# A two-block transformer kernel on one core: the first half's attention placed ahead of the state space inputs, scan and far projections

## What is computed

```python
h = rms_norm(concat([meta, x]), pre_mix_g)          # 16 + 1024 tokens
q1, q2, k1, k2, v, u = split(h @ w_in)              # four 64-wide heads, two branches each; u is 512 wide
q1, q2, k1, k2 = rope(...)
o = softmax(q1 k1) v - lam * softmax(q2 k2) v       # causal, then rms_norm
# state space model, 32 groups of 16 channels, 64 complex states each
x_t = A x_{t-1} + B u_t                              # scan over all 1040 tokens
y_t = Re(C x_t) + D u_t                              # then gelu, gate, rms_norm
x = x + rms_norm(concat([o, y]) @ w_out)             # then a gated feed-forward
# block two: retention | RWKV-7 | feed-forward | per-layer gate
for t in tokens:                                     # RWKV-7, 8 heads of 64
    sa = S @ (-kk_t)
    S = S * w_t + outer(sa, b_t) + outer(v_t, k_t)
    y_t = S @ r_t
```

## Time and profile before

| | us |
|---|---|
| median of 3 runs | 3780.99 (3775.95 to 3783.14) |
| the profiled execution | 3778.1 |
| its span, first to last instruction | 3776.3 |
| PE busy, share of span | 3229.1, 86% |
| DVE | 1729.2, 46% |
| ACT | 940.8, 25% |
| POOL | 1967.0, 52% |

### The profile page before, as it was taken

How to read it: one execution, slowest core, us unless ns; L and a number is a source line. 1 busy time by engine, 2 the same in 40 slices (tenths; PEclk the granted TensorE clock), 3 DMA queues, 4 the chain that set the end, 5 groups by cost and what they waited for, 6 DMA issues and landing times.

```text
span 3776.3 us, 48065 instructions
## 1 busy us (share of the span) xinstructions
PE 3229.1 (86%) x19536; PEld 2501.1 (66%) x19536; DVE 1729.2 (46%) x2399; ACT 940.8 (25%) x1665; POOL 1967.0 (52%) x1076
## 2 busy tenths in 40 slices
PE   5975587769999786988999998898899998899997
PEld 3654355547677564766777776676677777677885
DVE  6214623344443263186655555266566456322233
ACT  3110111233233223113223322413223322210012
POOL 4234111325455463664656566474567665667773
PEclk9886687879999897998999999999899999999998
DMA  3422122312222232422222214332222221322221
GB/s 110 84 79 71 51 61 61 102 67 69 83 67 67 73 134 101 146 92 70 68 71 78 72 61 157 111 118 84 70 67 83 77 83 64 123 84 94 95 96 62
DMA packets 144364, 321.57 MB, mean 85 GB/s; under 512 B 25904, under 2 KB 62960, under 8 KB 144144
## 3 DMA queue, kind: packets, MB, share of 16 engines
q1 hardware_dynamic: 58752, 213.94, 17.5%
q10 hardware_dynamic: 85392, 104.57, 8.8%
HBM read 277.68 MB, written 40.76 MB: 84 GB/s over the span
## 4 chain that ended last, share of the span: by engine, by line
PE 73%; DVE 16%; ACT 4%; ACTq 2%; issue 2%; DMA 2%; POOL 1%; DVEq 0%; POOLq 0%
PE ps L1680 29%; PE ps L1709 12%; PE ps L1721 11%; PE ps L1911 3%; PE ps L1455 3%; PE ps L1544 2%; DVE acc_dense L2088 1%; DVE act_lo L2088 1%; DVE ffh_lo L2761 1%; PE ps L1572 1%; ACTq L883 1%; DVE xn_dense L2095 1%; DVE local L2088 1%; DVE rq L2088 1%; PE ps L1618 1%
## 5 line engine op out<-in xcount | busy, mean ns | idle before, releaser
L522 POOL TENSOR_TENSOR w_hi<-w_raw,ones 128x1024 fp32r<-128x1024 f32 x408 | 799.3, 1959 | 1406.4 <-DMA w_raw<-weights 1392.2
L524 POOL TENSOR_TENSOR w_lo<-w_raw,w_hi 128x1024 fp32r<-128x1024 f32 x408 | 1005.7, 2465 | 32.0
L1680 PE MATMUL ps<-act_hi,w_hi 128*128 128x512 f32 x1696 | 711.1, 419 | 7.2 <-DVE act_lo L2088 6.6
L1680 PE MATMUL ps<-act_lo,w_hi 128*128 128x512 f32 x1696 | 685.2, 404 | 0.0
L1680 PE MATMUL ps<-act_hi,w_lo 128*128 128x512 f32 x1696 | 680.7, 401 | 0.0
L1680 PEld LDWEIGHTS ps<-act_hi,w_hi 128*128 128x128 f32 x1696 | 328.5, 194 | 100.9 <-issue 15.7
L1680 PEld LDWEIGHTS ps<-act_hi,w_lo 128*128 128x128 f32 x1696 | 327.7, 193 | 76.7
L1680 PEld LDWEIGHTS ps<-act_lo,w_hi 128*128 128x128 f32 x1696 | 327.9, 193 | 67.9 <-issue 1.7
L2088 DVE TENSOR_TENSOR acc_dense<-acc_dense,ps 128x512 f32<-128x512 f32 x352 | 241.9, 687 | 242.3 <-PE ps L1709 182.3
L1709 PE MATMUL ps<-w_hi,ffh_hi 128*128 128x512 f32 x704 | 298.0, 423 | 57.0 <-DVE acc_dense L2088 54.9
L626 ACT ACT_TABLE_LOAD x204 | 261.7, 1283 | 295.0 <-PE ps L1680 104.8
(11 more groups left out here) (381 smaller groups left out, 4765.2 us busy)
## 6 DMA issues: line engine op xcount, KB each, us to landing
w_raw<-weights SPq DMA_DIRECT2D x408, 512.0 KB, 3.5
rw<-rw_t ACTq DMA_DIRECT2D x24, 256.0 KB, 2.4
rw<-lora_t ACTq DMA_DIRECT2D x24, 256.0 KB, 2.0
row<-x ACTq DMA_DIRECT2D x8, 512.0 KB, 3.6
row_dense<-x ACTq DMA_DIRECT2D x8, 512.0 KB, 3.9
res<-row_dense ACTq DMA_DIRECT2D x8, 512.0 KB, 2.6
row_mix<-res ACTq DMA_DIRECT2D x8, 512.0 KB, 6.8
res<-row_mix ACTq DMA_DIRECT2D x8, 512.0 KB, 4.6
```

Of the source, the lines that this page charges most:

```text
L522: pool.tensor_tensor(w_hi[:, s], raw, ones[:, 0:1].to_broadcast([P, 1024]), MUL).then_inc(w_hi_made, 1)
L524: pool.tensor_tensor(w_lo[:, s], raw, w_hi[:, s].bitcast(F32), SUB).then_inc(w_ready, 1)
L1680: mm = pe.matmul(out, ws[w][:, s, P * k:P * k + P], acts[a][:, k, x], start=(k, w, a) == (0, 0, 0), stop=(k, w, a) == (KT - 1, 1, 0))
```

## The change

- `PROJ` keeps `v` and the near q and k pieces. All of `u` moves into `FAR`, in front of the far `v` and q, k: 12 pieces of `u`, 4 of `v`, 8 of q and k. The near pieces of attention come first in the weight order.
- `ssm()`: the tables `g_t` are turned in the same 8 steps as `kd`, copied to `gt_out` and stored to memory (`gt_scratch`). The input steps, the scan and the output steps all run between steps of `attention(0)`: inputs at steps 18 to 25, scan at 26 to 36, first tables at 37, outputs at 38, 42, ... 66.
- `HEAD_EVENTS`: 8 far pieces ahead of step 0, two per step up to step 13, then 49 over the next 50 steps.
- `u_scratch` is stored in two parts per unit (66 and 64 columns of each of 8 phases), since the far half of `u` comes later. The gather of `u_in` is issued by ACT behind the first far `v` piece.
- One semaphore, `tables_stored`, for all three tables; `kd` and its banks are single, not double.
- RWKV: `rw_off_product` and `rw_merge` go round the four quarters of the array instead of two; one ACT copy of 512 columns (`zi`) takes the place of an ACT and a DVE copy of 256. `rw_parts` is reordered: 32 of its 48 products go round four quarters, 16 round two.

```diff
-    PROJ = ([("u", m, s) for m in range(4) for s in range(3)] + [("v", i, 0) for i in (*range(HALF), NT)]
-            + [("qk", m, s) for m in range(8) for s in spans_of(m)])
+    PROJ = [("v", i, 0) for i in (*range(HALF), NT)] + [("qk", m, s) for m in range(8) for s in spans_of(m)]
...
-    FAR = [("v", i) for i in range(HALF, NT)] + [("qk", m) for m in range(8)]
+    FAR = [("u", m, s) for m in range(4) for s in (0, 2)] + [("u", m, 1) for m in range(4)] + [("v", i, 1) for i in range(HALF, NT)] + [("qk", m, 1) for m in range(8)]
...
-    PROJ_EVENTS = ["proj", "ssm"] + ["proj"] * 3 + ["ssm", "proj"] * TB + ["proj"] * 3 + ["ssm", "ssm", "proj", "proj"] * TB
+    PROJ_EVENTS = ["proj", "ssm"] + ["proj"] * 5 + ["ssm", "proj"] * TB + ["proj"] * 5
...
-        events, done = ["heads"] + ["far"] * 3, 3
-        extra = [["ssm"]] * (SCAN_PARTS + 1) + ([[]] * 5 + [["ssm"]]) * TB
+        events, done = ["heads"] + ["far"] * 8, 8
+        extra = [[]] * 18 + [["ssm"]] * (TB + SCAN_PARTS + 2) + ([[]] * 3 + [["ssm"]]) * (TB - 1)
+        early = 14
         for n in range(ATT_STEPS - 1):
-            now = min(4 * len(FAR) + 1, 3 + (4 * len(FAR) - 2) * (n + 1) // (ATT_STEPS - 5))
+            now = 8 + 2 * (n + 1) if n < early else min(FAR_PIECES, 8 + 2 * early + (FAR_PIECES - 8 - 2 * early) * (n + 1 - early) // (ATT_STEPS - 5 - early))
...
                 elif kind == "v":
                     spills_landed(0)
                     act.wait_ge(*far_done(n))
-                    give(fn(v_o[:, :], ps[:, m % 2, :], ACT.Copy), proj_kept)
+                    give(fn(v_o[:, :], ps[:, n % 2, :], ACT.Copy), proj_kept)
                     spill(t["v_scratch"][m], v_o[:, :], 0)
+                    if n == FAR_U:
+                        spills_landed(0, 1)
+                        for e in range(OCT):
+                            act.dma_start(u_in[SG * e:SG * e + SG], t["u_scratch"][:, :, e, :].rearrange("m (g h) c -> h (m g) c", h=SG)).then_inc(ssm_landed, 16)
+                        load_input_factors(0)
...
-            chunk_products(1, (off16, n_t)[n], inv)
-            for u in range(4):
-                for c in range(2):
-                    mm = pe.matmul(ps[head(c), 7, CH * u:CH * u + CH], inv[head(c), u], ident[head(c), head(c)], start=True, stop=True)
+            for lhs, rhs, at in (((off16, n_t)[n], inv, 0), (inv, None, P)):
+                for j in range(2):
+                    for side in range(2):
+                        u = 2 * side + j
+                        for c in range(2):
+                            right = ident[head(c), head(c)] if rhs is None else rhs[head(c), u]
+                            mm = pe.matmul(ps[head(c ^ side), 5 + 2 * side, at + CH * j:at + CH * j + CH], lhs[head(c), u], right, start=True, stop=True)
...
-        def rw_off_product(v, n):
-            dve.wait_ge(rw_mm, nth("mm", f"z{n}", v))
-            mark(dve.tensor_copy(xt[0][:, :, :], units(bank(1, 0, 256))), rw_dve, nth("dve", f"z{n}", v))
```

More of the change, by code:

```diff
@@ L168, in proj_done, with ends_far @@
         if ends_unit(kind, m, s):
-            return unit_done, {"u": U_SSM + m, "v": U_V + 3, "qk": U_QK + m}[kind] + 1
+            return unit_done, AT[0, U_V + 3 if kind == "v" else U_QK + m] + 1
         return proj_psum, sum(not ends_unit(*p) for p in PROJ[:n + 1])
     PROJ_COUNT = sum(not ends_unit(*p) for p in PROJ)
+    def ends_far(kind, m, s):
+        return {"u": s == 1, "v": m == NT - 1, "qk": True}[kind]
     def far_done(n):
[L176 to L179, removed]
+        kind, m, _ = FAR[n]
+        if not ends_far(*FAR[n]):
+            return proj_psum, PROJ_COUNT + sum(not ends_far(*f) for f in FAR[:n + 1])
+        return unit_done, AT[{"u": (0, U_SSM + m), "v": (1, U_V + 3), "qk": (1, U_QK + m)}[kind]] + 1
     def rope_index(m, s):
@@ L690, in project @@
                 src = ps[:, n % 3, 0:c1 - c0]
[L691 to L705, removed]
+                if kind == "v":
+                    if n:
+                        spills_landed(0)
                     rows = META if m == NT else P
@@ L730, in project_far @@
             act.dma_start(rope[:, :, 0:BANK], t["rope"][:, :, NEAR:L]).then_inc(const_landed, 16)
[L731 removed]
+            for n, (kind, m, s) in enumerate(FAR):
                 if kind == "qk" and m >= 2:
                     store_far(m - 2)
[L734 to L736 removed]
+                if s != 2:
+                    for part in range(3):
+                        yield
+                if kind == "u":
+                    if s != 2:
+                        spills_landed(m % 2)
+                    act.wait_ge(*far_done(n))
+                    c0, c1 = SPANS[s]
+                    o0, o1 = {0: (META // OCT, NEAR // OCT), 1: (0, BANK // OCT), 2: (0, META // OCT)}[s]
+                    src = ps[:, n % 2, 0:c1 - c0].rearrange("p (c s) -> p c s", s=OCT)
+                    give(fn(u_t[:, m % 2, :, o0:o1].rearrange("p s c -> p c s"), src, ACT.Copy), proj_kept)
+                    if s:
+                        first, last = (0, NEAR // OCT) if s == 2 else (NEAR // OCT, NOCT)
+                        spill(t["u_scratch"][m][:, :, first:last], u_t[:, m % 2, :, 0:last - first], m % 2)
+                elif kind == "v":
                     spills_landed(0)
                     act.wait_ge(*far_done(n))
[L739 removed]
+                    give(fn(v_o[:, :], ps[:, n % 2, :], ACT.Copy), proj_kept)
                     spill(t["v_scratch"][m], v_o[:, :], 0)
+                    if n == FAR_U:
[3 more added lines that the diff above has]
+                        load_input_factors(0)
                 else:
@@ L1428, in project_far, with far_inputs, far_values @@
             yield
-        def far_values(i, part):
+        def far_inputs(n, m, s, part):
+            pos, (c0, c1) = AT[0, U_SSM + m], SPANS[s]
+            if s == 0 and part == 0:
+                pe.wait_ge(w_ready, pos + 1)
+            for k in range(KT) if s == 2 else range(2 * part, 2 * part + 2):
+                for w, a in PASSES:
+                    mm = pe.matmul(ps[:, n % 2, 0:c1 - c0], ws[w][:, pos % SLOTS, P * k:P * k + P], acts[a][:, k, c0:c1],
+                                   start=(k, w, a) == (0, 0, 0), stop=(k, w, a) == (KT - 1, 1, 0))
+            if s == 2 or part == 3:
+                post(mm, unit_done if s == 1 else proj_psum)
+        def far_values(n, i, part):
             pos = AT[1, U_V + part]
```

203 lines of the change are left out of this document (112 added, 91 removed), and 2 rows, old and new, of the table STAGES.

## The result

| | us |
|---|---|
| before, median of 4 | 3778.47 |
| changed, median of 4 | 3675.9 (3667.09 to 3688.23) |
| ratio, 95% interval | 0.9728 (0.9704 to 0.9753) |
| changed once more, beside other runs of before | 0.9762 (0.9738 to 0.9787) |
| profiled execution: time, span | 3688.2, 3686.4 |

The change saves 103 us by the first comparison and 91 by the second. The forecast was 45, so the sign was right and the size under half of what came.

The account below looks back on a forecast made before the run. It took PE to bound the projection and RWKV, with DVE busy in the scan. Attention's end 32 us earlier and RWKV 13 less: 3778.1 - 32 - 13 = 3733, stated as 3734; range 3672 to 3772.

Parts of the forecast that it names:

- the gather: Attention: the wait from ACT's issue of the `u_in` loads to PE's first input product, 22 us.
- the gap from the projection's end to the first scores: Last rope, store and reload stay at 22.2 us, far pieces add some 6; first scores at 232 instead of 346.
- the scan: Attention steps 26 to 36: 94 us, about 10 of it from six POOL units beside it.
- the RWKV term: RWKV tiles: 160 passes over four quarters at 24.4 ns instead of 29.4 over two, 0.8 us a tile, 13 in all.
- Steps 39 to 68: Attention behind the scan: 7.5 units at 19 us each, 142 us, with more output work and one far piece more each.
- The end comes to 57.7 + 97.8 + 31 + 8 + 9 = 204: Projection's end: start, first stage's PE time, five more wide pieces, eight turnings, rotations; 204 us instead of 324.
- Eight input steps: Attention steps 18 to 25: product, two ACT copies, next table's load and attention's own step, 5 us each, 40.
- Steps 0 to 18: Attention's start: 66 us for steps 0 to 13 with two far pieces each, 16 us for steps 14 to 18.
- Steps 37, 38, table load with nine DMAs: Attention between the scan and the later outputs: 8 us.
- C: Rival, chance 0.20: attention packs better, far pieces fill PE's idle in the scan; attention ends at 562, total 3675 us.
- Rival B: RWKV: the array's quarters work in parallel, halving a pass; 38 us saved, total 3708; chance 0.15.
- Rival A: Attention: engines' lists hold each other, PE's clock stays near 0.5; attention ends at 714, total 3827, slower; chance 0.09.

Follow-up runs that it names:

- the two-line swap: Kernel before, with POOL's split of weight unit 8 + b put ahead of input table b in the projection instead of behind it: ratio 0.9935, 24 us less.

## Why the prediction was right and wrong

**Right:** the direction, the gather (22 and 22.2), the gap from the projection's end to the first scores (28 and 28.4), the scan (94 and 96.9, with POOL busy 22.8 us beside it), the chain of the stages, POOL's coupling as a cost of the old projection, and that a part of the gain ahead of the scores is given back in attention. It is less than forecast: of the 126 us that the first scores gain 51 are given back, not 82 of 114; attention takes 359 us, before 308.

**Right by luck:** the RWKV term, 13 forecast and 14 to 18 measured. Its step "24.4 ns each; over two ... 29.4" compared a group that stands alone with one from the middle of a run. A pass over four quarters costs 14.4 ns in the middle of a run, PE's busy time falls by 28 us, and 11 of these come back as PE's idle time, which the sum did not have. The floor of about 25 ns a start, which the prediction takes from the Trainium skill's page "TensorE: Matmul & The Clock Gate", section "Wait — 56ns, not 53.3ns?", and finds borne out by the 24.4, is not what this trace shows for products that take turns over four quarters.

**Wrong in size:** 32 us for everything ahead of RWKV, against 72 measured alone and 75 in the trace at the end of attention. The 41 us between 620 and 579.3, by terms:

- "Steps 39 to 68 ... I take 19 each" fell by most: 118.5 us and not 142. The working added a third of an output step and a far piece to a mean unit of before and took PE's busy time for the price of an output. That mean, 16.9 us, was itself made of outputs in bad places. `act_hi` in the changed kernel (timeline of ACT, six units apart):

```profile
465.57 0.28 ACT L633 ACTIVATE act_hi<-ps 128x128 fp32r<-128x128 f32 x1 [4.75 <-issue]
...
564.46 0.28 ACT L633 ACTIVATE act_hi<-ps 128x128 fp32r<-128x128 f32 x1 [4.76 <-issue]
```

  A unit takes 16.5 us with an output in every unit and one far piece more. The same six units took 17.6 before. The nine DMAs show here as ACT's 4.75 us, ahead of `act_hi`, for which PE doesn't wait at once. The change moved the outputs to the third step; the text of the diff says so (every fourth step from 38), and the prediction priced only how many there are. On the kernel before that place alone is worth 30 us in time (19 to 40) and 15 in the trace, so by an estimate 1.2 to 2.5 us a unit, 9 to 19 of these 23.5. The rest is argued: with outputs in the third step of the kernel before a unit takes 16.4 us, and the far piece more that the changed kernel adds to it shows no price.
- "The end comes to 57.7 + 97.8 + 31 + 8 + 9 = 204" was 12.3 us too late: the projection's last small piece ends at 191.7. The sum took the first stage's PE time and a price of 6.2 us a piece at that stage's granted clock of 0.81. Now PE is busy 129.8 of the 134.0 us and the clock is 0.90. By an estimate, the forecast's 146.3 us times 0.81 / 0.90 are 131.7.
- "Eight input steps ... 5 each", 8.5 us: 3.9 each, at a clock of 0.93. Steps 0 to 18: 7.5 us, for the same reason: PE had far pieces in a row and 0.93.
- "Steps 37, 38, table load with nine DMAs: 8" went the other way, 7.6 us longer. From the first issue to the first output product it takes 7.4 us, and the output's 24 products take 7.6 more, for which the 8 left no room.
- The scan came 2.9 us longer than forecast, but with other shares inside. Its largest group in both kernels, before and then after:

```profile
L2088 DVE TENSOR_TENSOR local<-xs,a_step 128x320 f32<-128x320 f32 x24 | 16.9, 704 | 0.8
```

```profile
L2131 DVE TENSOR_TENSOR local<-xs,a_step 128x320 f32<-128x320 f32 x24 | 22.4, 934 | 0.8
```

  The same 24 operations take 934 ns on the mean and not 704. The six large groups of the scan together went from 50.8 to 67.3 us, 16.5 and not the 10 taken from one row. The cause is to be seen operation by operation. One of them beside a split, the split, and the same operation some 9 us later with POOL idle:

```profile
364.99 2.73 DVE L2131 TENSOR_TENSOR xs<-xs,local 128x320 f32<-128x320 f32 x1
```

```profile
364.69 2.47 POOL L531 TENSOR_TENSOR w_lo<-w_raw,w_hi 128x1024 fp32r<-128x1024 f32 x1
```

```profile
373.58 0.74 DVE L2131 TENSOR_TENSOR xs<-xs,local 128x320 f32<-128x320 f32 x1
```

  Every operation of these groups that takes far more than its usual time overlaps one of POOL's splits, and all that stand clear of them take 0.49 to 0.74 us. No run took POOL away from the scan.

These terms make up the 41 us: 23.5, 12.3, 8.5 and 7.5 less, 7.6 and 2.9 more, and 0.6 more in the gap and the gather.

The first rival that matters is C, with 0.20: it asked for units at 17 (16.5 came), inputs at 30 (31.5), and an end at 562 (579). It was nearest, for the reason of packing that it gave in part, but its gather of 12 us and its scan of 82 (96.9) did not come. That its time of 3675 is the first median, 3675.9, is partly luck; the second comparison's was 3685.9. (The range's lower end, called C's time, is given as 3672, and C's own sum is 3675.) Rival B was right on the price of a pass and wrong on what it brings. Rival A's mechanism, a list that holds another engine and a clock that falls with it, is real, as the run with the outputs in the second step shows; the changed kernel does not meet it there.

## What to carry to other kernels

Where DMA issues share an engine's list with a short chain that another engine waits for, their place within the repeating unit decides, more than their number: five microseconds of issue are free behind the norm and dear ahead of it. Before a mean time per unit is scaled to another schedule, sort the units by what stands where in them. Take the price of a short product from the middle of a run of its like, and ask what PE will wait for once it is faster: here a third or more of what it saved came back as idle time. When waits ahead of a stretch go, price its matmuls at a higher clock, not at the old one. And before a large reordering is judged, try the two-line swap in the old kernel: alone it gave 24 us there, a quarter of what the whole change gave.

## What the runs showed of the hardware

Short waits of PE cost more than their length: where only the place of nine DMA issues differed, PE was idle 11.6 us more in the stretch to attention's end and busy 21.0 us more with the same matmuls, at a mean granted clock of 0.74 against 0.85. Products of 64x64 that go round the four quarters of the array cost 14.4 ns a pass in the middle of a run, those that go round two 29.4. A DVE operation of 0.74 us took 2.73 beside a split of POOL. ACT needs 0.45 to 0.5 us for each of these issues, and up to 2.3 us for the gather's last ones, whose line reads:

```profile
L752 ACTq DMA_DIRECT2D u_in<-u_scratch x8: 341/509/2327, 294.6 to 301.5; - x8
...
DMA to landing us min/median/max: 4.9/11.6/14.9
```

The scratch store of `u` in rows of 264 bytes, which could have let it land sooner, left these numbers as they were in the earlier trace rows.
